# Loading w_hi once for 512 activation columns in a fused attention, mLSTM and SwiGLU layer

## The chip, the cores and the metric

The kernel runs on one core of one Trainium2 chip. The metric is the device time of one execution in microseconds; the profile is of one execution, and its span goes from the first to the last instruction.

## The reference

One layer on 256 tokens of width 1024, all in fp32:

```python
h = rms_norm(x, mix_norm_g)
q_a, k_a, v_a, q_m, k_m, v_m, o_m, i_m, f_m, g_a, g_m = split(h @ w_in)
y_a = causal_attention(q_a, k_a, v_a, slopes)              # 8 heads of 64, one block
q_m, k_m = split(silu(causal_depthwise_conv([q_m, k_m], conv_qk)))   # 4 taps
y_m = head_layer_norm(mlstm(q_m, k_m, v_m, i_m, log_sigmoid(f_m)) * sigmoid(o_m)) * mlstm_norm_g
merged = sigmoid(g_a) * (y_a @ w_out_attn) + sigmoid(g_m) * (y_m @ w_out_mlstm)
x = x + merged @ w_o
h = rms_norm(x, ffn_norm_g)
x = x + (silu(h @ w_ffn_gate) * (h @ w_ffn_up)) @ w_ffn_down         # hidden width 2816
out = rms_norm(x, final_norm_g)
```

## The kernel before

Every large product is made of three matmuls in the type fp32r. An fp32 number is split into a rounded part hi and the remainder lo, and w x is summed as w_hi x_hi + w_hi x_lo + w_lo x_hi. The weights come in chunks of 2048 columns on 128 partitions (1 MB), numbered c in the order in which they are used. Each chunk passes through four engines:

- SyncE issues its load into one of three buffers `w_raw`, after the split of chunk c-3 is done (`lo_ready`).
- ScalarE copies it to `w_hi` (`split_hi`, L404, in the FFN loop L636); it waits for the load and for chunk c-6 to be used, since `w_hi` and `w_lo` are rings of six.
- VectorE subtracts and writes `w_lo` (`split_lo`, L670, in the FFN loop L975).
- TensorE uses it and raises `chunk_used`.

Each engine has its own program, written out by hand, and works through it strictly in order. In the projection ScalarE and VectorE run one loop over c: in iteration c they do what belongs to the middle of the layer at that point, then split chunk c+4, then read the results of a chunk.

The chunks of the projection (L1152 and following), 22 in all:

- 0 to 3: q_m and k_m, feature-major. `tap3` (ScalarE) writes the last convolution tap into `qk_m`, `conv` (VectorE) adds the three others, each of them reading the sum in PSUM. After chunk 1 TensorE does the small product for the eight gate columns (`gates`). In iteration 2, ahead of its split and of `conv(2)`, VectorE works out the gate rows: additions, a wait for ScalarE's exponential and logarithm, two scans (L832 to L852).
- 4 to 7: q_a and k_a, feature-major, copied out by ScalarE (`copy_qk`). After chunk 5 TensorE spreads the gate rows (`gate_columns`); VectorE's iteration 4 begins with a copy that waits for it (L854).
- 8 to 13: v_a, v_m and o_m, token-major, two chunks each. The o block is read by ScalarE with a sigmoid in iteration 15, after the last softmax (`read_block(6, ...)`).
- 14 to 21: the two merge gates, feature-major, read by ScalarE with a sigmoid (`read_gate`).

Between the chunks TensorE does the small matmuls of attention and mLSTM; `scores(3)` stands before chunk 15, `numerators(h)` behind chunks 15 to 18. VectorE's `head_out(h)` follows each of these, and in iteration 19 the normalisation of all heads (L897 to L905), which waits for GpSimd.

A feature-major chunk (`feature_chunk`) holds 8 x 2 weight tiles of 128 x 128. Each tile is the stationary operand, the 256 tokens are the moving one:

```python
for f in range(2):
    o = bank[:, f * S:(f + 1) * S]
    for k in range(KT):
        mm(o, hi[:, w], hT_hi[:, k, :], start=(k == 0), stop=False)
        mm(o, hi[:, w], hT_lo[:, k, :], start=False, stop=False)
        ins = mm(o, lo[:, w], hT_hi[:, k, :], start=False, stop=(k == KT - 1))
```

The chunk's 2 x 256 columns fill one PSUM bank. The projection goes round the four banks of `pp`, so chunk c follows chunk c-4 in its bank: chunk 4 waits for `conv(0)`, chunk 5 for `conv(1)`, and so on (L1173, L1175). The attention works in the four banks of `pa`. A token-major product (`token_product`) has the activations stationary and 512 weight columns moving.

Chunks 22 to 25 are the two out-projections, in the order attention, mLSTM (columns 0 to 511), attention, mLSTM (columns 512 to 1023): the first two go to the four banks of `pa`, the others to `pp`. VectorE multiplies them with the gates and adds (`merge_attention`, `merge_mlstm`), ScalarE and VectorE split the result (`merged_hi`, `merged_lo`). Chunks 26 to 29 are w_o. Then the FFN: a first group of 256 hidden features token-major, then ten groups feature-major (`group`), each with a gate chunk, an up chunk and the down product of the group before. The gate sums alternate between banks 0 and 1 of `pa`, the up sums between 2 and 3. ScalarE takes the silu of the gate, VectorE multiplies by the up sum, and both split the product (`hidden`).

Of the kernel before, what the change touches and what calls it, by code (L numbers as in the profile page):

```python
# [60 lines left out]

def build(nc, x, mix_norm_g, w_in, conv_qk, b_igate, b_fgate, mlstm_norm_g, w_out_attn,
# [11 lines left out]
    with ExitStack() as ctx:  # L74
# [62 lines left out]
        wif = yT_hi[:, :, :].rearrange("p f n -> p (f n)")[:, 0:KT * 100].rearrange("p (k n) -> p k n", k=KT)  # L137
# [9 lines left out]
        sel_r = yT_lo[0:36, 0:2, :].rearrange("p f n -> p (f n)")  # L147
        m_rows = yT_lo[0:36, 2, :]
# [84 lines left out]
        hid_turned = sem("hid_turned")  # L233
        prod_done = sem("prod_done")
# [10 lines left out]
        block = ctx.enter_context(nc.Block())  # L245

# [151 lines left out]
        def _(act):  # L398
# [112 lines left out]
            for c in range(C_OUT):  # L511
# [62 lines left out]
                elif c > 2 * GATES:  # L574
                    read_gate(c - 1)
# [83 lines left out]
        def _(dve):  # L659
# [169 lines left out]
            for c in range(C_OUT):  # L829
# [77 lines left out]
                if c < 4:  # L907
                    conv(c)
# [446 lines left out]
```

## Time and profile before

| what | value |
|---|---|
| median of 3 runs | 401.44 us |
| lowest, highest | 400.5, 401.46 us |
| span of the profiled execution, which is what the profile gives as its own time | 399.2 us |
| TensorE matmuls, share of the span | 387.7 us, 97% |
| TensorE weight loads | 360.9 us, 90% |
| VectorE | 226.0 us, 57% |
| ScalarE | 188.2 us, 47% |
| GpSimd | 36.2 us, 9% |
| mean granted TensorE clock | 0.994 |

Weight loads run beside matmuls. Busy time of a matmul is from its start to its modelled end, and successive matmuls overlap, so their rate is read from their starts. A releaser is what ended an engine's idle time.

### The profile page before, as it was taken

The page shows a single profiled execution, that of the slowest core. Times are in us where ns is not written, and L with a number is a line of the kernel's source. Part 1 is how long each engine was busy: PE and PEld are TensorE (multiplying, and loading weights), DVE is VectorE, ACT ScalarE, POOL GpSimd, SP SyncE. Part 2 cuts the span into 40 slices and gives each one's busy share as a digit, 9 for nine tenths or more (in the row PEclk, how much of TensorE's full clock was granted, in tenths as well). Part 3 has the DMA queues.
Part 4 walks back from the last instruction along what each step waited for, and adds up shares of the span by engine and source line. Part 5 has one row for each costly group of instructions (what it writes and reads, how often), then busy time and mean ns, then how long its engine had stood idle before and what let it go on. Part 6 is the DMA issues. An engine that isn't in the chain of part 4 may idle for free.

```text
span 399.2 us, 6572 instructions
## 1 busy us (share of the span) xinstructions
PE 387.7 (97%) x2749; PEld 360.9 (90%) x2749; DVE 226.0 (57%) x282; ACT 188.2 (47%) x224; POOL 36.2 (9%) x47
## 2 busy tenths in 40 slices
PE   6999999999999999999999999999999999999992
PEld 5799998777999999998899999999999999999982
DVE  1788857648529577587547572552816437263024
ACT  4772996454575445243446353350624416152003
POOL 2897010000000010000100000000000000000002
PEclk9999999999999999999999999999999999999997
DMA  7996276844535489635336665729366292730002
GB/s 266 318 316 211 78 238 223 262 151 120 191 111 181 141 314 318 213 117 196 106 105 225 215 224 182 240 81 313 102 213 205 110 309 65 256 105 0 0 0 105
DMA packets 52620, 71.13 MB, mean 178 GB/s; under 512 B 2260, under 2 KB 41208, under 8 KB 52600
## 3 DMA queue, kind: packets, MB, share of 16 engines
q1 hardware_dynamic: 52456, 70.57, 53.8%
q8 instruction: 16, 0.26, 0.3%
q10 hardware_dynamic: 144, 0.26, 0.2%
q14 instruction: 4, 0.03, 0.0%
HBM read 69.78 MB, written 1.05 MB: 177 GB/s over the span
## 4 chain that ended last, share of the span: by engine, by line
PE 93%; DMA 2%; ACT 1%; SPq 1%; DVE 1%; issue 0%; POOLq 0%; POOL 0%; ACTq 0%
PE pa L1021 10%; PE pa L1020 10%; PE pa L1019 10%; PE pp L1027 9%; PE pp L1028 9%; PE pp L1029 9%; PE pp L1019 7%; PE pp L1020 7%; PE pp L1021 7%; DMA w_raw<-in_w_in 2%; PE pa L1027 2%; PE pa L1029 2%; PE pa L1028 2%; PE pp L1247 1%; PE pp L1246 1%; PE pp L1245 1%
## 5 line engine op out<-in xcount | busy, mean ns | idle before, releaser
L670 DVE TENSOR_TENSOR w_lo<-w_raw,w_hi 128x2048 fp32r<-128x2048 f32 x38 | 86.5, 2289 | 37.3 <-ACT w_hi L404 37.3
L1019 PE MATMUL pa<-hT_hi,w_hi 128*128 128x256 f32 x320 | 90.6, 283 | 0.0
L1021 PE MATMUL pa<-hT_hi,w_lo 128*128 128x256 f32 x320 | 90.6, 283 | 0.0
L1020 PE MATMUL pa<-hT_lo,w_hi 128*128 128x256 f32 x320 | 90.6, 283 | 0.0
L404 ACT ACTIVATE w_hi<-w_raw 128x2048 fp32r<-128x2048 f32 x38 | 72.7, 1915 | 16.8 <-DMA w_raw<-in_w_in 8.3
L1019 PE MATMUL pp<-hT_hi,w_hi 128*128 128x256 f32 x240 | 68.8, 287 | 0.1
L1020 PE MATMUL pp<-hT_lo,w_hi 128*128 128x256 f32 x240 | 67.9, 283 | 0.0
L1021 PE MATMUL pp<-hT_hi,w_lo 128*128 128x256 f32 x240 | 67.9, 283 | 0.0
L1020 PEld LDWEIGHTS pa<-hT_lo,w_hi 128*128 128x128 f32 x320 | 61.4, 192 | 0.4
L1019 PEld LDWEIGHTS pa<-hT_hi,w_hi 128*128 128x128 f32 x320 | 61.4, 192 | 0.3
L1021 PEld LDWEIGHTS pa<-hT_hi,w_lo 128*128 128x128 f32 x320 | 61.4, 192 | 0.0
L975 DVE TENSOR_TENSOR w_lo<-w_raw,w_hi 128x2048 fp32r<-128x2048 f32 x24 | 53.6, 2287 | 8.9 <-ACT w_hi L636 8.9
L636 ACT ACTIVATE w_hi<-w_raw 128x2048 fp32r<-128x2048 f32 x24 | 45.0, 1906 | 3.7 <-PE pp L1029 3.7
L1019 PEld LDWEIGHTS pp<-hT_hi,w_hi 128*128 128x128 f32 x240 | 46.0, 192 | 0.6 <-issue 0.3
L961 DVE TENSOR_TENSOR region_a<-pa,region_a 128x512 f32<-128x512 f32 x10 | 6.9, 692 | 69.3 <-PE pa L1021 69.3
L1020 PEld LDWEIGHTS pp<-hT_lo,w_hi 128*128 128x128 f32 x240 | 46.0, 192 | 0.0
L1021 PEld LDWEIGHTS pp<-hT_hi,w_lo 128*128 128x128 f32 x240 | 46.0, 192 | 0.0
L1027 PE MATMUL pp<-w_hi,yT_hi 128*128 128x512 f32 x88 | 34.4, 390 | 0.0
L1028 PE MATMUL pp<-w_hi,yT_lo 128*128 128x512 f32 x88 | 34.4, 390 | 0.0
L1029 PE MATMUL pp<-w_lo,yT_hi 128*128 128x512 f32 x88 | 34.2, 389 | 0.0
L624 ACT ACTIVATE yT_hi<-region_a 128x512 fp32r<-128x512 f32 x10 | 6.3, 633 | 56.7 <-DVE region_a L961 56.7
L1027 PE MATMUL pp<-w_hi,hT_hi 128*128 128x512 f32 x64 | 25.6, 399 | 0.0
(190 smaller groups left out, 575.7 us busy)
## 6 DMA issues: line engine op xcount, KB each, us to landing
w_raw<-in_w_in SPq DMA_DIRECT2D x21, 1024.0 KB, 5.4
w_raw<-in_w_ffn_gate SPq DMA_DIRECT2D x11, 1024.0 KB, 5.3
w_raw<-in_w_ffn_up SPq DMA_DIRECT2D x11, 1024.0 KB, 6.1
w_raw<-in_w_ffn_down SPq DMA_DIRECT2D x11, 1024.0 KB, 6.6
w_raw<-in_w_o SPq DMA_DIRECT2D x4, 1024.0 KB, 6.0
w_raw<-in_w_out_attn SPq DMA_DIRECT2D x2, 1024.0 KB, 5.0
w_raw<-in_w_out_mlstm SPq DMA_DIRECT2D x2, 1024.0 KB, 5.6
x_sb<-in_x SPq DMA_DIRECT2D x2, 512.0 KB, 3.8
```

What stands on the lines that cost most here:

```text
L404: nc.scalar.activation(w_hi[:, slot_of(c), :], w_raw[:, c % RAW, :], ACT.Copy).then_inc(hi_ready, 1)
L624: nc.scalar.activation(yT_hi[:, 2 * (g % 2):2 * (g % 2) + 2, :], hid[:, g % 2, :].rearrange("p (f n) -> p f n", f=2), ACT.Copy).then_inc(a ...
L636: nc.scalar.activation(w_hi[:, slot_of(c + r), :], w_raw[:, (c + r) % RAW, :], ACT.Copy).then_inc(hi_ready, 1)
L670: nc.vector.tensor_tensor(w_lo[:, slot_of(c), :], w_raw[:, c % RAW, :], w_hi[:, slot_of(c), :].bitcast(F32), ALU.subtract).then_inc(lo_rea ...
L961: nc.vector.tensor_tensor(hid[:, g % 2, :], pa[:, 2 + g % 2, :], hid[:, g % 2, :], ALU.mult).then_inc(prod_done, 1)
L975: nc.vector.tensor_tensor(w_lo[:, slot_of(c + r), :], w_raw[:, (c + r) % RAW, :], w_hi[:, slot_of(c + r), :].bitcast(F32), ALU.subtract).t ...
L1019: mm(o, hi[:, w], hT_hi[:, k, :], start=(k == 0), stop=False)
L1020: mm(o, hi[:, w], hT_lo[:, k, :], start=False, stop=False)
L1021: ins = mm(o, lo[:, w], hT_hi[:, k, :], start=False, stop=(k == KT - 1))
L1027: mm(o, aT_hi[:, k, tok], w_hi[:, s, w], start=start, stop=False)
L1028: mm(o, aT_lo[:, k, tok], w_hi[:, s, w], start=False, stop=False)
L1029: return mm(o, aT_hi[:, k, tok], w_lo[:, s, w], start=False, stop=stop)
```

## The change

`hT` and `yT` now hold hi and lo side by side, so that one matmul with the weights w_hi takes 512 moving columns, x_hi and x_lo, and writes two sums into the two halves of a bank. A second matmul adds w_lo x_hi to the first half. At reading, ScalarE copies the second half out of PSUM and VectorE adds the first half to it. This holds for the feature-major chunks of the projection, for three of the four out-projection chunks and for the ten FFN groups.

A feature-major chunk now fills two banks. The projection has two pairs of banks (`pair_of`), and a chunk waits until the previous use of its pair is read (`proj_free`, `earlier_uses`): chunks 2 to 7 for the sum of chunk c-2, chunk 15 for the reads of the o block, chunks 16 and 17 for the sums of 14 and 15, and so on. `conv`, `sum_qk` and `sum_gate` do the additions on VectorE, behind the split of chunk c+4 in iteration c, those of the gate chunks one iteration later. `tap3` and the convolution taps read the sum from SBUF; `tap3(c)` comes in ScalarE's iteration c+1, ahead of that iteration's split and, in iteration 2, ahead of its exponential. The sigmoid of a gate is a step of its own (`open_gate`).

In the out-projection both attention chunks use `pa` and both mLSTM chunks `pp`. In the FFN the gate always uses banks 0 and 1 of `pa`, the up chunk 2 and 3, so the next gate waits for the addition of the one before (`gate_summed`, `up_summed`). The first FFN group takes gate and up weights in one matmul of 512 columns.

```diff
+def pair_of(c):
+    return c % 2 if c < 2 * FEATURE_MAJOR else (c // 2) % 2 if c < 2 * GATES else (c + 1) % 2
+def earlier_uses(c):
+    first = [n for n in range(c) if n < 2 * FEATURE_MAJOR or n >= 2 * GATES or n % 2 == 0]
+    return sum(pair_of(n) == pair_of(c) for n in first)
...
-        hT_hi = sb("hT_hi", [P, KT, S], F32R)
-        hT_lo = sb("hT_lo", [P, KT, S], F32R)
-        yT_hi = sb("yT_hi", [P, 8, S], F32R)
-        yT_lo = sb("yT_lo", [P, 8, S], F32R)
+        hT = sb("hT", [P, KT, 2, S], F32R)
+        hT_hi, hT_lo = hT[:, :, 0, :], hT[:, :, 1, :]
+        yT = sb("yT", [P, 8, 2, S], F32R)
+        yT_hi, yT_lo = yT[:, :, 0, :], yT[:, :, 1, :]
...
+        def gate_part(c):
+            n = c - 2 * GATES
+            return (region_a, region_b)[n // 4][:, 512 * (n % 4):512 * (n % 4 + 1)]
+        def main_sum(q):
+            return pp[:, 2 * q:2 * q + 2, 0:S]
+        def rest_sum(q):
+            return pp[:, 2 * q:2 * q + 2, S:2 * S]
...
+            def read_rest(c, dst):
+                act.wait_ge(chunk_used, c + 1)
+                nc.scalar.activation(dst, rest_sum(pair_of(c)), ACT.Copy).then_inc(rest_read, 1)
             def tap3(c):
                 b, h = divmod(c, 2)
-                act.wait_ge(chunk_used, c + 1)
+                act.wait_ge(proj_free[pair_of(c)], c // 2 + 1)
                 if c == 0:
                     act.wait_ge(vcol_set, 1)
                 for f in range(2):
                     ft = 4 * b + 2 * h + f
                     col = 4 + 3 * 8 + ft
-                    ins = nc.scalar.activation(qk_m[:, ft, :], pp[:, 2 * (b % 2) + h, f * S:(f + 1) * S],
-                                               ACT.Copy, scale=vcol[:, col:col + 1])
+                    ins = nc.scalar.activation(qk_m[:, ft, :], raw[:, c, f, :], ACT.Copy, scale=vcol[:, col:col + 1])
                 ins.then_inc(tap3_done, 1)
...
+            def read_mix(n):
+                act.wait_ge(chunk_used, C_OUT + n + 1)
+                if n == 2:
+                    act.wait_ge(merged, 1)
+                dst = (mix_sum, ml_sum)[n % 2].rearrange("p (f n) -> p f n", f=4)
+                nc.scalar.activation(dst, (pa, pp)[n % 2][:, :, S:2 * S], ACT.Copy).then_inc(mix_rest, 1)
+            def open_gate(c):
+                act.wait_ge(proj_free[pair_of(c)], earlier_uses(c) + 1)
+                part = gate_part(c)
+                nc.scalar.activation(part, part, ACT.Sigmoid).then_inc(gate_read, 1)
...
+                if c in (1, 2):
+                    tap3(c - 1)
...
+                if c in (3, 4):
+                    tap3(c - 1)
...
-                    tap3(c)
+                    read_rest(c, raw[:, c])
                 elif c < 8:
-                    copy_qk(c)
+                    ft = 4 * (c // 2 - 2) + 2 * (c % 2)
+                    read_rest(c, qk_a[:, ft:ft + 2, :])
                 elif c == 9:
                     read_block(4, lambda t: va[:, t], ACT.Copy)
                 elif c > 2 * GATES:
-                    read_gate(c - 1)
+                    read_rest(c - 1, gate_part(c - 1).rearrange("p (f n) -> p f n", f=2))
+                    if c > 2 * GATES + 1:
+                        open_gate(c - 2)
...
+                nc.scalar.activation(two(hid), pa[:, 0:2, S:2 * S], ACT.Copy).then_inc(gate_rest, 1)
+                act.wait_ge(chunk_used, i * 6 + (C_FFN + 3 * g + 1))
+                nc.scalar.activation(two(up_sum), pa[:, 2:4, S:2 * S], ACT.Copy).then_inc(up_rest, 1)
+                act.wait_ge(gate_summed, i * 2 + g)
+                nc.scalar.activation(hid[:, g % 2, :], hid[:, g % 2, :], ACT.Silu).then_inc(silu_f_done, 1)
...
+                q = pair_of(c)
+                dve.wait_ge(rest_read, c + 1)
+                nc.vector.tensor_tensor(raw[:, c], main_sum(q), raw[:, c], ALU.add).then_inc(proj_free[q], 1)
...
+            def sum_qk(c):
+                q = pair_of(c)
+                ft = 4 * (c // 2 - 2) + 2 * (c % 2)
+                part = qk_a[:, ft:ft + 2, :]
+                dve.wait_ge(rest_read, c + 1)
+                nc.vector.tensor_tensor(part, main_sum(q), part, ALU.add).then_inc(proj_free[q], 1)
...
+            def sum_gate(c):
+                q = pair_of(c)
+                part = gate_part(c).rearrange("p (f n) -> p f n", f=2)
+                dve.wait_ge(rest_read, c - 5)
+                nc.vector.tensor_tensor(part, main_sum(q), part, ALU.add).then_inc(proj_free[q], 1)
...
             def merge_attention(n):
-                if n == 0:
-                    dve.wait_ge(proj_free[0], 10)
-                    dve.wait_ge(proj_free[1], 8)
-                dve.wait_ge(chunk_used, C_OUT + 2 * n + 1)
+                dve.wait_ge(gate_read, 2 * n + 2)
+                dve.wait_ge(mix_rest, 2 * n + 1)
+                total = mix_sum.rearrange("p (f n) -> p f n", f=4)
+                nc.vector.tensor_tensor(total, pa[:, :, 0:S], total, ALU.add).then_inc(mix_summed, 1)
+                dve.wait_ge(mix_summed, n + 1)
                 part = region_a[:, 1024 * n:1024 * (n + 1)]
-                nc.vector.tensor_tensor(part, (pa, pp)[n][:, 0:2, :].rearrange("p b n -> p (b n)"), part, ALU.mult)
+                nc.vector.tensor_tensor(part, mix_sum, part, ALU.mult)
             def merge_mlstm(n):
+                dve.wait_ge(gate_read, 2 * n + 6)
                 dve.wait_ge(chunk_used, C_OUT + 2 * n + 2)
                 for b in range(2):
                     part = slice(512 * (2 * n + b), 512 * (2 * n + b + 1))
-                    link(nc.vector.tensor_tensor(region_b[:, part], (pa, pp)[n][:, 2 + b, :], region_b[:, part],
-                                                 ALU.mult))
+                    total = main_sum(b)
+                    gate = region_b[:, part].rearrange("p (f n) -> p f n", f=2)
+                    if n == 0:
+                        dve.wait_ge(mix_rest, 2)
+                        summed = ml_sum[:, 512 * b:512 * (b + 1)].rearrange("p (f n) -> p f n", f=2)
+                        link(nc.vector.tensor_tensor(summed, total, summed, ALU.add))
+                        total = summed
+                    link(nc.vector.tensor_tensor(gate, total, gate, ALU.mult))
...
+                elif c < 8:
+                    sum_qk(c)
+                elif c > 2 * GATES:
+                    sum_gate(c - 1)
...
+                dve.wait_ge(gate_rest, i * 2 + g)
+                nc.vector.tensor_tensor(two(hid), pa[:, 0:2, 0:S], two(hid), ALU.add).then_inc(gate_summed, 1)
+                dve.wait_ge(up_rest, i * 2 + g)
+                nc.vector.tensor_tensor(two(up_sum), pa[:, 2:4, 0:S], two(up_sum), ALU.add).then_inc(up_summed, 1)
                 dve.wait_ge(silu_f_done, i * 2 + g + 1)
-                dve.wait_ge(chunk_used, i * 6 + (C_FFN + 3 * g + 1))
-                nc.vector.tensor_tensor(hid[:, g % 2, :], pa[:, 2 + g % 2, :], hid[:, g % 2, :], ALU.mult
+                dve.wait_ge(up_summed, i * 2 + g)
+                nc.vector.tensor_tensor(hid[:, g % 2, :], up_sum[:, g % 2, :], hid[:, g % 2, :], ALU.mult
...
+            def split_product(bank, hi, lo, xT, k, start, stop):
+                mm(bank, hi, xT[:, k], start=start, stop=False)
+                return mm(bank[:, 0:S], lo, xT[:, k, 0, :], start=False, stop=stop)
+            def feature_chunk(c, banks):
                 s = slot_of(c)
                 hi, lo = w_hi[:, s, :], w_lo[:, s, :]
                 for f in range(2):
-                    o = bank[:, f * S:(f + 1) * S]
                     for k in range(KT):
                         w = slice(k * 256 + f * P, k * 256 + (f + 1) * P)
-                        mm(o, hi[:, w], hT_hi[:, k, :], start=(k == 0), stop=False)
-                        mm(o, hi[:, w], hT_lo[:, k, :], start=False, stop=False)
-                        ins = mm(o, lo[:, w], hT_hi[:, k, :], start=False, stop=(k == KT - 1))
+                        ins = split_product(banks[f], hi[:, w], lo[:, w], hT, k, k == 0, k == KT - 1)
                 return ins
...
                 elif b < FEATURE_MAJOR or b >= GATES:
-                    if b >= GATES:
-                        pe.wait_ge(proj_free[b % 2], 2 * (b // 2 - 1) - 1 + h)
-                    elif b >= 2:
-                        pe.wait_ge(conv_step, 6 * (c - 3))
-                    if c == 1:
-                        pe.wait_ge(vcol_set, 1)
-                    feature_chunk(c, pp[:, 2 * (b % 2) + h, :]).then_inc(chunk_used, 1)
+                    q = pair_of(c)
+                    if c > 1:
+                        pe.wait_ge(proj_free[q], earlier_uses(c))
+                    feature_chunk(c, (pp[:, 2 * q, :], pp[:, 2 * q + 1, :])).then_inc(chunk_used, 1)
...
-                banks = (pa, pp)[n]
                 for m in range(2):
+                    banks = (pa, pp)[m]
                     if n == 0 and m == 0:
                         pe.wait_ge(ya_lo_set, 4)
                         pe.wait_ge(num_read, H_M)
+                        pe.wait_ge(ym_lo_set, 2)
                     elif n == 0:
-                        pe.wait_ge(ym_lo_set, 2)
-                    elif m == 0:
                         pe.wait_ge(proj_free[0], 10)
+                        pe.wait_ge(proj_free[1], 9)
                     else:
-                        pe.wait_ge(proj_free[1], 8)
+                        pe.wait_ge((mix_summed, merged)[m], 1 + m)
                     c = C_OUT + 2 * n + m
                     s = slot_of(c)
                     pe.wait_ge(lo_ready, c + 1)
...
                         pe.wait_ge(m_lo_set, 2 * h + 2)
+                        pe.wait_ge(mix_summed, 2)
...
+                    w = (slice(None), slice(s, s + 2), slice(256 * k, 256 * (k + 1)))
+                    o = pa[:, 2 + t, :]
+                    mm(o, hT_hi[:, k, tok], w_hi[w], start=(k == 0), stop=False)
+                    mm(o, hT_lo[:, k, tok], w_hi[w], start=False, stop=False)
+                    ins = mm(o, hT_hi[:, k, tok], w_lo[w], start=False, stop=(k == KT - 1))
+                    if t == 0 and k == 4:
+                        turn(rb_t[:, 1], (pp[:, 0, :], pp[:, 1, :]), 6)
...
-                        pe.wait_ge((silu_f_done, prod_done)[r], i * 2 + (g - 1))
-                    feature_chunk(c + r, pa[:, 2 * r + g % 2, :]).then_inc(chunk_used, 1)
+                        pe.wait_ge((gate_summed, up_summed)[r], i * 2 + (g - 1))
+                    elif r == 1:
+                        pe.wait_ge(prod_done, 1)
+                    feature_chunk(c + r, (pa[:, 2 * r, :], pa[:, 2 * r + 1, :])).then_inc(chunk_used, 1)
```

## Rows read from the trace of the kernel before

**Rows 1.** The page, first part: busy time, share of the span and instructions
```profile
PE 387.7 (97%) x2749; PEld 360.9 (90%) x2749; DVE 226.0 (57%) x282; ACT 188.2 (47%) x224; POOL 36.2 (9%) x47
```

**Rows 2.** The table of waits for TensorE: total, times, longest
```profile
PE pa L1038 <- DVE region_b L800: 2.0, 1, 2.0
```

**Rows 3.** Timeline of TensorE, 299 to 304 us: start, duration, line, shapes
```profile
299.79 0.39 PE L1028 MATMUL pp<-w_hi,yT_lo 128*128 128x512 f32 x1
...
301.60 0.28 PE L1019 MATMUL pa<-hT_hi,w_hi 128*128 128x256 f32 x1
...
303.99 0.28 PE L1021 MATMUL pa<-hT_hi,w_lo 128*128 128x256 f32 x1
```

**Rows 4.** Costliest groups by line and shape: count, busy, mean ns, idle before
```profile
L1019 PE MATMUL pa<-hT_hi,w_hi 128*128 128x256 f32 x320 | 90.6, 283 | 0.0
...
L1019 PE MATMUL pp<-hT_hi,w_hi 128*128 128x256 f32 x240 | 68.8, 287 | 0.1
...
L620 ACT ACTIVATE region_a<-pa 128x512 f32<-128x512 f32 x10 | 6.0, 597 | 39.0 <-PE pa L1021 39.0
...
L777 DVE TENSOR_TENSOR region_b<-pp,region_b 128x512 f32<-128x512 f32 x2 | 1.4, 688 | 0.6 <-PE pp L1247 0.6
...
L770 DVE TENSOR_TENSOR region_a<-pa,region_a 128x1024 f32<-128x1024 f32 x1 | 1.2, 1224 | 1.1 <-PE pa L1247 1.1
```

**Rows 5.** Timeline of VectorE, 26 to 46 us
```profile
26.37 2.36 DVE L670 TENSOR_TENSOR w_lo<-w_raw,w_hi 128x2048 fp32r<-128x2048 f32 x1 [1.28 <-ACT w_hi L404]
28.65 2.42 DVE L691 SCALAR_TENSOR_TENSOR region_a<-pp,vcol,region_a 128x255 f32<-128x255 f32 x6
...
35.53 0.46 DVE L834 TENSOR_SCALAR o_sb<-pa,b_if 4x256 f32<-4x256 f32 x1
...
40.30 0.41 DVE L843 SCALAR_TENSOR_TENSOR o_sb<-o_sb 4x256 f32<-4x256 f32 x1 [2.21 <-ACT o_sb L522]
...
43.96 2.29 DVE L670 TENSOR_TENSOR w_lo<-w_raw,w_hi 128x2048 fp32r<-128x2048 f32 x1
```

**Rows 6.** Timeline of ScalarE, 26 to 30 us
```profile
26.24 0.82 ACT L431 ACTIVATE region_a<-pp,vcol 128x256 f32<-128x256 f32 x2
...
27.77 1.91 ACT L404 ACTIVATE w_hi<-w_raw 128x2048 fp32r<-128x2048 f32 x1
```

**Rows 7.** Timeline of TensorE: what stands at the places the prediction speaks of
```profile
8.95 1.32 PE L1038 MATMUL pa<-ident,region_b 128*128 128x128 f32 x8 [2.03 <-DVE region_b L800]
...
26.81 0.28 PE L1019 MATMUL pp<-hT_hi,w_hi 128*128 128x256 f32 x1
...
49.94 0.73 PE L1065 MATMUL pa<-yT_lo 36*128 36x256 f32 x4
...
50.94 0.38 PE L1019 MATMUL pp<-hT_hi,w_hi 128*128 128x256 f32 x1
...
110.82 0.38 PE L1019 MATMUL pp<-hT_hi,w_hi 128*128 128x256 f32 x1
...
139.78 0.36 PE L1019 MATMUL pp<-hT_hi,w_hi 128*128 128x256 f32 x1
...
391.71 0.39 PE L1029 MATMUL pp<-w_lo,yT_hi 128*128 128x512 f32 x1
```

**Rows 8.** Timeline of ScalarE, 115 to 117 us: the reads of the o block
```profile
115.67 1.09 ACT L463 ACTIVATE o_sb<-pp 128x512 f32<-128x512 f32 x2
```

**Rows 9.** Timeline of VectorE, 140 to 147 us
```profile
140.06 0.16 DVE L743 SCALAR_TENSOR_TENSOR den<-pa,rcol 128x2 f32<-128x2 f32 x1 [2.23 <-PE pa L1139]
...
144.20 2.14 DVE L903 TENSOR_SCALAR o_sb<-o_sb,mv,lnr 128x128 f32<-128x128 f32 x8 [2.13 <-POOL lnr L392]
```

**Rows 10.** Windows: busy time of the five engines, granted clock, DMA share, GB/s
```profile
8.00:12.00 4.00, 2.87 (x17) 1.81 (x17) 3.63 (x6) 2.36 (x4) 0.73 (x1) 1.00 1.10 361
...
393.00:394.00 1.00, 0.00 (x0) 0.00 (x0) 1.00 (x2) 0.59 (x2) 0.26 (x1) 1.00 0.27 102
394.00:395.00 1.00, 0.00 (x0) 0.00 (x0) 0.27 (x2) 0.00 (x0) 0.84 (x2) 0.52 0.43 160
```

More of the change, by code:

```diff
@@ L615, in hidden, with two @@
             def hidden(i, g):
+                def two(ap):
+                    return ap[:, g % 2, :].rearrange("p (f n) -> p f n", f=2)
                 act.wait_ge(chunk_used, i * 6 + (C_FFN + 3 * g))
@@ L919, in _ @@
             split_lo(C_WO)
+            sum_gate(C_OUT - 1)
             split_lo(C_WO + 1)
@@ L1156, in _ @@
                 if c == 0:
-                    hh, hl, lh = (w_hi, hT_hi), (w_hi, hT_lo), (w_lo, hT_hi)
-                    order = ((hh, 0), (hl, 0), (hh, 1), (hl, 1), (lh, 1), (lh, 0))
                     for f in range(2):
-                        for n, ((w_part, x_part), half) in enumerate(order):
-                            pe.wait_ge(((first_half_hi, hi_ready) if w_part is w_hi else
-                                        (first_half_lo, lo_ready))[half], 1)
-                            pe.wait_ge(hT_hi_set if x_part is hT_hi else hT_lo_set, 3 + half)
+                        w = [slice(k * 256 + f * P, k * 256 + (f + 1) * P) for k in range(KT)]
@@ L1166, in _ @@
+                        for half in range(2):
+                            pe.wait_ge((first_half_hi, hi_ready)[half], 1)
+                            pe.wait_ge(hT_lo_set, 3 + half)
                             for k in range(4 * half, 4 * half + 4):
-                                ins = mm(pp[:, 0, f * S:(f + 1) * S],
-                                         w_part[:, 0, k * 256 + f * P:k * 256 + (f + 1) * P], x_part[:, k, :],
-                                         start=(n == 0 and k == 0), stop=(n == 5 and k == 3))
+                                mm(pp[:, f, :], w_hi[:, 0, w[k]], hT[:, k], start=(k == 0), stop=False)
@@ L1170, in _ @@
+                        for half in (1, 0):
+                            pe.wait_ge((first_half_lo, lo_ready)[half], 1)
+                            for k in range(4 * half, 4 * half + 4):
+                                ins = mm(pp[:, f, 0:S], w_lo[:, 0, w[k]], hT_hi[:, k, :], start=False,
+                                         stop=(half == 0 and k == 3))
                     ins.then_inc(chunk_used, 1)
                 elif b < FEATURE_MAJOR or b >= GATES:
-                    if b >= GATES:
-                        pe.wait_ge(proj_free[b % 2], 2 * (b // 2 - 1) - 1 + h)
-                    elif b >= 2:
-                        pe.wait_ge(conv_step, 6 * (c - 3))
```

115 lines of the change are left out of this document (61 added, 54 removed).

## The prediction

> **What bounds the kernel now.** I began with the busy shares. TensorE has work for 387.7 of 399.2 us, VectorE and ScalarE for about half of it [rows 1]; the table of waits gives TensorE's matmuls one wait of 2.0 us in the norm at the start and nothing that matters later [rows 2]. So the kernel is as long as its matmuls, and a gain has to come out of their spacing. The timeline of TensorE gives that spacing, start to start: the eight 512-column matmuls from 299.79 to 301.60 take 0.226 us each, the twenty 256-column ones from 301.60 to 303.99 take 0.1195 us each [rows 3]. Doubling the columns adds 0.107 us, so each matmul carries about 12.7 ns that do not depend on its columns (2 x 0.1195 - 0.2263).
>
> Then I read VectorE's and ScalarE's timelines, because the change makes TensorE wait for them [rows 5 to 9]. Both run a fixed program in order, and in the first 55 us and around the last gate chunks VectorE is far behind TensorE. Nobody sees it today: with four banks in turn, chunk 4 waits only for the convolution of chunk 0, and chunk 6 for that of chunk 2.
>
> **What is saved.** A triple of 256-column matmuls becomes one of 512 columns and one of 256: 0.346 instead of 0.359 us, 12.7 ns less. Of such triples there are 256 in the 16 feature chunks of the projection (240 in the rows and the 16 of chunk 0, which has a line of its own), 320 in the FFN loop [rows 4] and 48 in three of the four out-projection chunks (4 x 4 weight tiles each, by the code). That is 624 x 12.7 ns = 7.9 us. The first FFN group turns 96 matmuls of 256 columns into 48 of 512: 0.6 us. Together 8.5 us, 0.2 us for each chunk, if a mixed sequence keeps both spacings. The Trainium skill (TensorE: Matmul & The Clock Gate, Back-to-back issue gap) states N/2.4 + 2.5 ns for a warm isolated matmul; by that the 672 matmuls saved would be worth an estimated 1.7 us. The rows show 12.7 ns, and the sum goes by them.
>
> **What is added.** Each bank pair needs a ScalarE copy (0.6 us, as other 512-column copies here) and a VectorE add (0.69 us, as the 512-element operations of L777 [rows 4]). Neither engine is short of time in the sum. What counts is when a pair is free. A chunk now takes two banks, two pairs go round, and chunk c waits for the sum of chunk c-2, which stands in VectorE's program behind the split of chunk c+2. I follow that program with the durations of before.
>
> *Chunk 2.* The gate matmuls now end near 26.6 (26.81 less 0.2 [rows 7]). The sum of chunk 0 can start only after the split that runs to 28.65 [rows 5], so it ends at 29.35. Stall 2.8 us.
>
> *Chunk 3.* tap3 now reads the sum, so it starts at 29.4 and takes 0.8 (ScalarE's 0.82 pair); the split of chunk 5 on ScalarE moves behind it, to 32.0 [rows 6]. VectorE: taps 30.25 to 32.65, split 34.9, sum of chunk 1 at 35.6. TensorE ends chunk 2 at 34.95. Stall 0.65 us. Chunk 3 ends at 41.15.
>
> *Chunk 4.* It needs the sum of chunk 2. Ahead of that on VectorE stand tap3(1) by ScalarE (to 36.4), taps (to 38.85), then the whole gate-row block, from 35.53 to 40.30 and on to 43.96 in the rows [rows 5], 8.4 us with ScalarE's exponential, table load and logarithm inside it: to 47.25. Then the split of chunk 6, 2.3: 49.55. Then the sum: 50.25. Stall 9.1 us. Even without any delay upstream the sum could not be there before 46.95 (the split that starts at 43.96 ends at 46.25), so this wait doesn't hang on small errors.
>
> *Chunk 5.* tap3(2) waits for that sum, then the split on ScalarE (to 52.85), VectorE's taps and split (55.75) and the sum: 56.45, TensorE is there at 55.8. Stall 0.65.
>
> *Chunk 6.* VectorE's next instruction is the copy of the gate columns (0.17 us), which waits for TensorE's small matmuls behind chunk 5 (1.0 us, 49.94 to 50.94 [rows 7]), then split 8 and the sum of chunk 4: 0.17 + 2.29 + 0.69. Stall 3.2 us. Chunks 7 to 14: sums in time by 1 us or more, no stall; there the shift is 14 to 15 us.
>
> *Chunk 15.* It shares its pair with the o block. Today it goes to another bank and starts at 110.82 [rows 7], as the scores of the last head pair end. Now it waits for both sigmoid reads of the o block, which ScalarE does after the last softmax and a table load, until 116.76 (115.67 + 1.09) [rows 8]. Stall 5.9 us.
>
> *Chunks 16 to 19.* Head output, split and sum take 5.0 us after the numerators, a chunk 5.55: no stall. *Chunk 20* needs the sum of chunk 18. In the rows VectorE has head output from 140.06, a wait for GpSimd, and the normalisation to 146.3; then split 2.2 and sum 0.7: 149.2 [rows 9]. TensorE would be there at 139.78 + 5.76 = 145.55 [rows 7]. Stall 3.7 us.
>
> *Out-projection.* The fourth chunk waits for the merge of the second: copy 1.1, twice 0.69 x 3, in all 5.3, against the third chunk of 5.55: just hidden. But the merge runs on into the w_o product: from the end of the second chunk VectorE and ScalarE need 1.1 + 4.2 + 1.4 (low halves) + 2.25 (split) + 1.2 + 1.2 (sum, product of 1024 [rows 4]) + 2.25 + 2.8 + 1.4 = 17.85 us, TensorE 5.55 + 5.76 + 5.45 = 16.75. Stall about 1.2 with semaphores. Its cover before was about 1.1 us.
>
> *FFN.* Here I charge nothing. ScalarE already waits 3.9 us for each gate chunk (39.0 in all [rows 4]), so it and VectorE arrive in time. The gate's sum is ready 1.4 us after its chunk and needed 11 us after; the up chunk's sum too. The hidden values come 1.4 us later than now and have two chunks and more as cover; the last group has one down product of 5.4 us over a chain of 3.5. The reads before chunk 0 shift too: 512-column matmuls need both halves of h, 0.7 us later, but chunk 1 starts with its own split at 19.07 as now.
>
> Stalls: 2.8 + 0.65 + 9.1 + 0.65 + 3.2 + 5.9 + 3.7 + 1.2 = 27.2 us. Less 8.5: +18.7 us.
>
> **The clock.** TensorE's last matmul ends near 392.1 and the granted clock, 1.00 (2.4 GHz) until 394, is 0.52 in the microsecond after it, which is the lower level, 1.2 GHz; the pause of 2.0 us before 8.95 left it at 1.00 [rows 2, 7, 10]. So stalls above about 2 us can put it at half, above all the four of 3.2, 9.1, 5.9 and 3.7 us. How long it stays there once matmuls run again no row shows. Bounds: nothing, and a whole chunk at half speed, 5.5 us more, after each of the four: 22 us. I take the return to be about as slow as the fall, 2 to 3 us of work at half speed, which loses 1.5 us per stall: 6.0, less 0.65 that falls into the wait of chunk 5: 5.3 us. The Trainium skill (TensorE: Matmul & The Clock Gate, The HAM clock gate) says the same in kind: idle halves the clock and sustained work gives it back; the fall in rows 10 agrees.
>
> **Sum.** 18.7 + 5.3 = +24.0 us. The durations are of an execution with span 399.2; the median of the runs is 401.44, 2.2 above, which I take as unchanged: 401.4 + 24.0 = 425.4, say 425.
>
> **The rivals.**
> 1. *Forecast:* VectorE's late sums hold TensorE, mainly at chunks 4, 15, 6 and 20, and the clock falls in most of these. 425, own range 421 to 430. Chance 0.66.
> 2. *Same waits, clock stays up or returns at once.* For it: the 2 us pause did nothing. Against it: 9.1 us is four times as long. 401.4 + 18.7 = 420. Chance 0.14.
> 3. *Same waits, clock slow for whole chunks.* 401.4 + 18.7 + 22 = 442. Chance 0.07.
> 4. *The saving is not there.* The mixed sequence could space as before, because a matmul's fixed part moves to the following one. 401.4 + 27.2 + 5.3 = 434; with 1.7 us saved 432. Against it: both spacings show the same fixed part. Chance 0.06.
> 5. *Fewer waits:* one of the chains is shorter than I read, most likely that of chunk 15 or of chunk 20 (5.9 and 3.7, with their clock cost 3): 412 to 413. Chance 0.04.
> 6. *The other side, faster.* TensorE stays fed, as in the FFN it will, and all 8.5 us count: 393. It would need the sum of chunk 2 to be ready when chunk 3 ends. The kernel is faster only if all stalls stay under 8.5 us; as chunk 4 alone cannot start before 46.95 where TensorE could be there at 37.7, the first 50 us would already have used it up. Chance 0.03, for an error in reading the order.
>
> Under 0.3% (1.2 us) nothing can be told from no change. Faster 0.03, within it 0.01, slower 0.96. The range takes rivals 1 and 2 with most of 4: 416 to 433.
>
> **What the profile after would show.** The table of waits should have TensorE rows released by VectorE additions: about 9 us before chunk 4, then 3 each at chunks 2 and 6, 4 at chunk 20, 1 in the w_o product, and 6 us released by the ScalarE sigmoid read. Chunks without a wait should take 5.55 us (0.226 + 0.120 per weight tile), an FFN group 0.4 us less than its 96 x 0.1195 + 24 x 0.2263 = 16.9. The FFN loop should have no TensorE wait; one there would be worth ten times its size and is the quickest way to make this too low. The windows after each long stall should show a clock under 1.00 for 2 to 3 us. It is too high if VectorE's first 50 us run faster than now, or if the clock never falls.

## The result, and the profile after

The changed kernel takes 433.4 us (433.28 to 434.76, 4 runs) where the kernel before takes 401.4 (400.5 to 401.46, 4 runs): a ratio of 1.0815 [1.0795, 1.0835]. It is 32.0 us slower. I had forecast 24 us slower, 425, with a range of 416 to 433, so it lies just outside.

The page of the changed kernel, its span, busy shares and granted clock, answers to [rows 1]:

```profile
span 431.2 us, 5314 instructions
PE 395.8 (92%) x2077; PEld 334.7 (78%) x2077; DVE 254.8 (59%) x322; ACT 208.1 (48%) x259; POOL 36.6 (8%) x47
PEclk9988798999997999699999999999999999999998
PE 78%; DVE 10%; ACT 4%; DMA 4%; issue 2%; SPq 1%; POOL 1%; POOLq 0%; DVEq 0%; ACTq 0%
```

TensorE is now busy for 92% of the span, not 97, and VectorE holds 10% of the chain that ended last. The row PEclk has a dip in the slices behind each long wait. Next is the table of waits of TensorE's matmuls, which answers to [rows 2] (columns: us in total, times, longest):

```profile
PE pp L1109 <- DVE region_b L741: 10.9, 2, 7.5
PE pp L1109 <- ACT o_sb L498: 6.0, 1, 6.0
PE pp L1109 <- DVE region_b L768: 3.6, 1, 3.6
PE pp L1109 <- DVE region_b L761: 3.2, 1, 3.2
...
PE pa L1125 <- DVE hT L866: 0.7, 1, 0.7
```

L1109 is the wide matmul of a feature chunk. L741 is the sum of a convolution chunk (it releases chunks 2 and 4), L498 the sigmoid read of the o block (chunk 15), L768 the sum of chunk 18 (chunk 20), L761 the sum of chunk 4 (chunk 6). These are the five chunks named before the run, with the releasers named. VectorE's timeline shows why the largest comes (start, duration, idle before and its releaser); it answers to [rows 5]:

```profile
26.38 2.29 DVE L726 TENSOR_TENSOR w_lo<-w_raw,w_hi 128x2048 fp32r<-128x2048 f32 x1 [2.09 <-ACT w_hi L437]
28.59 0.68 DVE L741 TENSOR_TENSOR region_b<-pp,region_b 128x512 f32<-128x512 f32 x1
...
39.57 0.47 DVE L916 TENSOR_SCALAR o_sb<-pa,b_if 4x256 f32<-4x256 f32 x1
...
44.08 0.41 DVE L925 SCALAR_TENSOR_TENSOR o_sb<-o_sb 4x256 f32<-4x256 f32 x1 [2.21 <-ACT o_sb L560]
...
47.74 2.29 DVE L726 TENSOR_TENSOR w_lo<-w_raw,w_hi 128x2048 fp32r<-128x2048 f32 x1
50.06 0.69 DVE L741 TENSOR_TENSOR region_b<-pp,region_b 128x512 f32<-128x512 f32 x1
```

The gate rows begin at 39.57 and end at 47.7, then comes the split of chunk 6, and only then the sum of chunk 2, which ends at 50.75. The prediction had 50.25. TensorE's timeline shows what the wait does to the matmuls behind it:

```profile
50.90 0.76 PE L1109 MATMUL pp<-hT,w_hi 128*128 128x512 f32 x1 [7.46 <-DVE region_b L741]
51.46 0.41 PE L1110 MATMUL pp<-hT,w_lo 128*128 128x256 f32 x1
...
54.88 0.63 PE L1109 MATMUL pp<-hT,w_hi 128*128 128x512 f32 x1
55.30 0.32 PE L1110 MATMUL pp<-hT,w_lo 128*128 128x256 f32 x1
55.47 0.40 PE L1109 MATMUL pp<-hT,w_hi 128*128 128x512 f32 x1
55.70 0.28 PE L1110 MATMUL pp<-hT,w_lo 128*128 128x256 f32 x1
55.82 0.39 PE L1109 MATMUL pp<-hT,w_hi 128*128 128x512 f32 x1
```

A wide matmul is charged 0.63 us and a pair takes 0.64 (start to start) until 55.4, then 0.40 and 0.35. The windows of 5 us after the waits give the granted clock in the column behind POOL. In four of them it is 0.50 or 0.51, the lower level, 1.2 GHz, as in [rows 10]; in 70:75 it is 0.75, as the clock comes back in the middle of that window:

```profile
30.00:35.00 5.00, 5.00 (x17) 4.31 (x16) 4.75 (x7) 2.50 (x3) 4.73 (x4) 0.51 0.60 204
50.00:55.00 5.00, 4.10 (x13) 3.55 (x14) 4.00 (x9) 3.19 (x4) 0.00 (x0) 0.50 0.64 213
70.00:75.00 5.00, 5.00 (x25) 4.30 (x24) 2.89 (x2) 3.58 (x3) 0.78 (x2) 0.75 0.50 176
135.00:140.00 5.00, 4.55 (x14) 3.90 (x15) 2.86 (x3) 2.59 (x3) 0.00 (x0) 0.50 0.02 3
175.00:180.00 5.00, 4.36 (x13) 3.76 (x14) 5.00 (x4) 2.43 (x2) 0.00 (x0) 0.50 0.79 248
```

By the timeline the slow stretches last 5.3, 4.5, 3.6, 5.2 and 5.9 us: 24.5 us in which work is done at 0.35/0.64 of the speed, so about 11 us lost. The 2.4 of them behind chunk 2 only shorten the waits of chunks 3 and 4, which VectorE sets, and 0.6 behind chunk 4 takes the place of a wait of chunk 5: some 8 net.

The FFN loop has no TensorE wait. Its pairs, at 2.4 GHz, answer to [rows 3]:

```profile
300.04 0.39 PE L1109 MATMUL pa<-hT,w_hi 128*128 128x512 f32 x1
300.27 0.28 PE L1110 MATMUL pa<-hT,w_lo 128*128 128x256 f32 x1
300.38 0.40 PE L1109 MATMUL pa<-hT,w_hi 128*128 128x512 f32 x1
...
301.09 0.40 PE L1109 MATMUL pa<-hT,w_hi 128*128 128x512 f32 x1
```

From 300.38 to 301.09 two pairs take 0.71 us. The period of a group, from one first gate matmul to the next, is 16.79 us (300.04 to 316.83), where before it was 16.98 (301.60 to 318.58). I had expected 0.4 less; it is 0.19, so 0.19/32 = 5.9 ns for each of a group's 32 pairs, not 12.7.

In the projection the same sequence has two paces. These are two pairs of chunk 14, 0.69 us, which is the 0.346 a pair of the forecast:

```profile
123.80 0.39 PE L1109 MATMUL pp<-hT,w_hi 128*128 128x512 f32 x1
...
124.49 0.39 PE L1109 MATMUL pp<-hT,w_hi 128*128 128x512 f32 x1
```

Chunks 16 and 18 keep that pace too, while chunks 17, 19 and 21, with the same code, take 0.353 or 0.354.

One more difference stands behind TensorE's last matmul. The last output transfer, which ScalarE issues, takes 0.9 us longer. This is its row in the table of transfers, before and after; the last number is the time from issue to landing:

```profile
out_x<-region_b ACTq DMA_DIRECT2D x1, 256.0 KB, 2.7
```

```profile
out_x<-region_b ACTq DMA_DIRECT2D x1, 256.0 KB, 3.6
```

The edit doesn't touch this transfer, and no run shows why it is slower. It takes 3.6 us in `warm`, `early`, `front_only` and `gates_only` as well and 2.7 in the four other experiments.

### The profile page after: what moved, and what is told of

The parts are those of the page before. It is cut to its first block, busy times and chain, and to the rows that moved or that the text cites. A ratio compares the mean times of both kernels' runs of the same rounds, so it can differ in the third digit from the quotient of the medians.

```text
span 431.2 us, 5314 instructions
## 1 busy us (share of the span) xinstructions
PE 395.8 (92%) x2077; PEld 334.7 (78%) x2077; DVE 254.8 (59%) x322; ACT 208.1 (48%) x259; POOL 36.6 (8%) x47
## 4 chain that ended last, share of the span: by engine, by line
PE 78%; DVE 10%; ACT 4%; DMA 4%; issue 2%; SPq 1%; POOL 1%; POOLq 0%; DVEq 0%; ACTq 0%
PE pa L1109 18%; PE pp L1109 12%; PE pa L1110 9%; PE pp L1125 8%; PE pp L1127 8%; PE pp L1126 8%; PE pp L1110 6%; DMA w_raw<-in_w_in 4%; DVE w_lo L726 3%; DVE region_a L750 1%; ACT w_hi L437 1%; PE pa L1379 1%; PE pa L1381 1%; PE pa L1380 1%; DVE region_a L861 1%
## 5 line engine op out<-in xcount | busy, mean ns | idle before, releaser
L1109 PE MATMUL pp<-hT,w_hi 128*128 128x512 f32 x240 | 96.5, 438 | 23.7 <-DVE region_b L741 10.9
L1109 PE MATMUL pa<-hT,w_hi 128*128 128x512 f32 x320 | 113.5, 399 | 0.0
L1110 PE MATMUL pa<-hT,w_lo 128*128 128x256 f32 x320 | 89.8, 281 | 0.0
L1109 PEld LDWEIGHTS pp<-hT,w_hi 128*128 128x128 f32 x240 | 50.6, 211 | 37.2 <-DVE w_lo L726 18.7
L1110 PE MATMUL pp<-hT,w_lo 128*128 128x256 f32 x240 | 72.1, 300 | 0.0
L1109 PEld LDWEIGHTS pa<-hT,w_hi 128*128 128x128 f32 x320 | 60.1, 188 | 14.8
L1110 PEld LDWEIGHTS pa<-hT,w_lo 128*128 128x128 f32 x320 | 60.4, 189 | 0.4
L1110 PEld LDWEIGHTS pp<-hT,w_lo 128*128 128x128 f32 x240 | 50.7, 211 | 0.0
L1125 PE MATMUL pp<-w_hi,yT 128*128 128x512 f32 x88 | 34.6, 393 | 0.0
L1126 PE MATMUL pp<-w_hi,yT 128*128 128x512 f32 x88 | 34.3, 390 | 0.0
L1125 PE MATMUL pp<-w_hi,hT 128*128 128x512 f32 x64 | 25.6, 399 | 0.0
L1126 PE MATMUL pp<-w_hi,hT 128*128 128x512 f32 x64 | 24.9, 389 | 0.0
```

Source lines behind the costliest of these rows:

```text
L1109: mm(bank, hi, xT[:, k], start=start, stop=False)
L1110: return mm(bank[:, 0:S], lo, xT[:, k, 0, :], start=False, stop=stop)
L1125: mm(o, aT_hi[:, k, tok], w_hi[:, s, w], start=start, stop=False)
L1126: mm(o, aT_lo[:, k, tok], w_hi[:, s, w], start=False, stop=False)
```

## The experiments

Each ratio is to the kernel before on the same chip.

### The clock by itself

`warm` is the changed kernel with extra matmuls, whose results nobody reads, in front of the five waits, so that TensorE stays at work while VectorE and ScalarE are late.

```diff
+filler = {2: (3, 14), 4: (3, 38), 6: (0, 13), 15: (1, 25), 20: (2, 15)}
 for c in range(C_OUT):
...
+    for _ in range(filler[c][1]):
+        mm(pa[:, filler[c][0], :], hT_hi[:, 0, 0:P], hT[:, 0], start=True, stop=True)
```

> The changed kernel with filler matmuls on TensorE ahead of the waits of chunks 2, 4, 6, 15 and 20 (14, 38, 13, 25 and 15 of 512 columns into banks that nothing reads), so that it is busy while it would wait; the sums come no earlier. Theory: the late sums are one cost and the clock's fall in the waits another, of about 11 us (what the chunks behind the five long waits took over their usual length in the trace of the changed kernel, against the 5.3 us of the prediction). Then the granted clock stays at 1.00, the chunks behind the waits take 5.65 us, and the time falls from 433.4 to 421 to 424 us. Rival: the chunks behind the waits were slow for another reason, and the half clock beside them costs nothing by itself because VectorE sets the pace there; then it stays at 431 to 434 us, with the waits longer by what the chunks are shorter.

Measured: 425.7 us (425.49 to 427.42), 1.0621 [1.0595, 1.0648], granted clock 0.996. The return from half speed costs 433.4 - 425.7 = 7.7 us. That is less than the 11 I had expected to get back, because part of the slow stretches had only filled waits, and so the time lies above the 421 to 424 expected. From the start of chunk 1 to that of chunk 21 the two traces differ by 8.1 us (166.7 and 158.6). TensorE's timeline of `warm` around chunk 4:

```profile
42.25 8.80 PE L1257 MATMUL pa<-hT 128*128 128x512 f32 x38
51.39 0.47 PE L1109 MATMUL pp<-hT,w_hi 128*128 128x512 f32 x1 [0.34 <-DVE region_b L741]
51.69 0.28 PE L1110 MATMUL pp<-hT,w_lo 128*128 128x256 f32 x1
51.81 0.40 PE L1109 MATMUL pp<-hT,w_hi 128*128 128x512 f32 x1
```

Filler and wait end 9.14 us after 42.25, when the chunk could have started; the forecast was 9.1. With the clock up, this kernel shows the waits that the sum was about. From the starts of the chunks, forecast in brackets: chunk 2 3.3 (2.8), chunk 3 1.1 (0.65), chunk 4 9.1 (9.1), chunk 5 0.6 (0.65), chunk 6 3.2 (3.2), chunk 15 6.1 (5.9), chunk 20 3.8 (3.7), w_o 0.9 (1.2). Together 28.1 against 27.2. So the waits were right, and the rival with whole chunks at half speed, 22 us, is out.

### The waits, moved away one group at a time

`early` puts the sums, and ScalarE's copies that go before them, where their data are ready: those of chunks 2 to 6 ahead of the gate rows, the taps or the split, the sum of chunk 18 ahead of the normalisation, the read of the o block ahead of the last softmax. `front_only` and `gates_only` have one half of this each.

```diff
 if c == 2:
+    sum_raw(2)
     dve.wait_ge(gates_done, 1)
...
+    sum_raw(3)
...
+if c in (3, 4, 5):
+    sum_qk(c + 1)
...
+read_block(6, lambda t: o_t[:, t], ACT.Sigmoid)
 ya_hi(1)
 softmax_exp(3)
-read_block(6, lambda t: o_t[:, t], ACT.Sigmoid)
...
 head_out(3)
+sum_gate(18)
 dve.wait_ge(lnr_set, 1)
```

> The changed kernel with the same work in another order: ScalarE's copies and VectorE's sums of chunks 2 to 6 stand ahead of the splits and of the gate rows instead of behind them, the sum of chunk 18 ahead of the normalisation of the heads, and the reads of the o block ahead of the last softmax. Theory: only the place of the sums in the queues makes TensorE wait. The wait of 7.5 us before chunk 4, of 6.0 before 15, of 3.6 before 20 and of 3.2 before 6 should be gone or under 1 us each, that before chunk 2 (3.4 us) stays and may cost 2 to 3 us of half clock behind it. Gain left from the wider matmuls: 672 x 6 to 7 ns, about 4.4 us. Sum: 401.4 - 4.4 + 3.4 + 2.5 + about 1.5 of small waits = 404, range 400 to 409. Rival: two bank pairs are too few wherever the sums stand, because the two copies per chunk load VectorE and ScalarE and other waits take their place; then 415 us or more.

Measured: 406.2 us (405.1 to 407.48), 1.0133 [1.0103, 1.0162], clock 0.993. The order alone takes 27.2 of the 32 us away. What is left in its table of waits:

```profile
PE pp L1123 <- DVE region_b L745: 4.7, 3, 3.0
...
PE pp L1123 <- DVE region_a L778: 1.2, 1, 1.2
PE pa L1139 <- DVE hT L876: 0.8, 1, 0.8
```

That is chunk 2 with 3.0 us, two of 0.8, one of 1.2 for the sum of a gate chunk and 0.8 in w_o, 6.7 us in all (7.4 from the starts), which is more than the 4.7 that the wide matmuls save. In this order, too, two pairs of banks don't feed TensorE.

> The changed kernel with the early sums of chunks 2 to 6 alone; chunks 15 and 20 wait as in the changed kernel. Theory: each wait costs its length and its own stretch of half clock and they add up. Gone: 7.5 (chunk 4) + 3.2 (chunk 6) of wait and 2.0 + 1.6 of slow matmuls behind them, 14.3 us; new small waits of about 2 us, as in the kernel with all sums early. 433.4 - 14.3 + 2 = 421 us, range 419 to 423. Rival: what is freed in front is given back at chunk 15 or 20 by queues that now have less time; then 424 us or more, with the waits there longer than 6.0 and 3.6.

Measured: 418.7 us (417.75 to 419.89), 1.0452 [1.0432, 1.0472]: 14.7 less than the changed kernel, and 0.3 under the range, since the 2 us of new small waits didn't come: chunk 5 waits 0.25 us. In the table of waits chunk 15 and chunk 20 keep theirs to the tenth:

```profile
PE pp L1123 <- ACT o_sb L498: 6.0, 1, 6.0
PE pp L1123 <- DVE region_b L779: 3.6, 1, 3.6
PE pp L1123 <- DVE region_b L746: 3.2, 2, 3.0
```

> The changed kernel with the other half alone: o block read ahead of the last softmax, sum of chunk 18 ahead of the normalisation. Gone: 6.0 + 3.6 of wait and 2.4 + 2.8 of slow matmuls behind them, 14.8 us: 418.6 us, range 417 to 421. Together with the run before the two gains should make up the 27.3 us of the kernel with all sums early. Rival: the two extra loads of ScalarE's function table and the sum in front of the normalisation move other waits; then less than 12 us are gained.

Measured: 422.0 us (421.35 to 422.66), 1.0531 [1.0514, 1.0549]: 11.4 less, and so above the range of 417 to 421; it is also under the 12 us that the rival named. The waits of chunks 15 and 20 are gone, but new ones stand in the table, and that of the convolution sums grew:

```profile
PE pp L1109 <- DVE region_b L740: 12.8, 2, 8.6
PE pp L1109 <- DVE region_b L760: 3.2, 1, 3.2
...
PE pp L1109 <- DVE region_a L767: 1.2, 1, 1.2
```

The 1.2 us is chunk 16, whose sum is the next to be late once chunk 15 is on time. The edit touches nothing before chunk 15, yet the waits there grew. VectorE's timeline of this profiled execution has two slow entries there:

```profile
30.99 3.54 DVE L749 SCALAR_TENSOR_TENSOR region_a<-region_b,vcol,region_a 128x255 f32<-128x255 f32 x6 [0.98 <-ACT region_a L469]
34.46 3.17 DVE L725 TENSOR_TENSOR w_lo<-w_raw,w_hi 128x2048 fp32r<-128x2048 f32 x1
```

In the changed kernel the same taps took 2.94 and the same split 2.28 us. With a weight load that came 0.7 us later this puts the chain to chunk 4 back by 2.0 us (52.90 instead of 50.90). What VectorE lost, GpSimd gained: its two instructions of L412, which run beside the split, took 2.44 us here and 3.67 in the traces of the changed kernel, `warm`, `early` and `front_only`, where the split took 2.28. That the two slow each other is my reading, and no run tests it. These 2.0 us and chunk 16's wait, 1.4 from its start, are the 3.4 that are missing from the 14.8 expected. Only one of the four executions has a trace; it was the fastest of them. Why the engines ran so here stays open. The two parts together gained 26.1, `early` 27.2: they add up within about a microsecond.

### The saving by itself

`ffn_only` is the kernel before with the change in the FFN loop and its first group alone; chunks 0 to 29 stay as they were.

```diff
-feature_chunk(c + r, pa[:, 2 * r + g % 2, :]).then_inc(chunk_used, 1)
+paired_chunk(c + r, (pa[:, 2 * r, :], pa[:, 2 * r + 1, :])).then_inc(chunk_used, 1)
```

> The kernel before with the FFN part of the change alone (512 columns in the ten groups and in the first one; projection and out-projection as before). Theory: no wait is added here and a pair of matmuls takes 0.353 us where the three took 0.360, so 320 x 6.5 ns + 48 x 13 ns = 2.7 us less: 398.7 us, ratio 0.993. Rival, the prediction's own term: 12.7 ns each, 4.7 us less: 396.7 us. Second rival: the groups gain nothing, since what a group saves is lost where TensorE waits for the next additions: 401.4 us.

Measured: 398.9 us (398.63 to 398.95), 0.994 [0.9924, 0.9957], period of a group 16.79 us, as in the changed kernel. As expected, this part alone is a gain, of 2.4 us. By the forecast's spacing it would have been 320 x 12.7 ns and 0.6, 4.7 us.

`ffn_grouped` runs the eight wide matmuls of a half chunk and then its eight narrow ones:

```diff
     for k in range(KT):
         w = slice(k * 256 + f * P, k * 256 + (f + 1) * P)
         mm(banks[f], hi[:, w], hT[:, k], start=(k == 0), stop=False)
+    for k in range(KT):
+        w = slice(k * 256 + f * P, k * 256 + (f + 1) * P)
         ins = mm(banks[f][:, 0:S], lo[:, w], hT_hi[:, k, :], start=False, stop=(k == KT - 1))
```

> As ffn_only, but in each half of a feature-major chunk the eight 512-column matmuls come first and then the eight of 256 columns, instead of in turn. If the alternation of the two widths is what makes a pair 0.353 us instead of 0.226 + 0.120 = 0.346, the groups lose another 32 x 6.5 ns = 0.2 us each and the time is 2.1 us under ffn_only, 396.6 us. Rival: the extra 6 to 7 ns belong to the 512-column matmul with activations of this layout (or to its weight load) wherever it stands; then the time is that of ffn_only within 0.3 us and the 512-column matmuls in a row are spaced by more than 0.226 us.

Measured: 397.0 us (396.69 to 397.07), 0.9894 [0.9877, 0.991], period 16.61. TensorE's timeline (successive matmuls of one kind are one entry):

```profile
299.64 1.07 PE L1053 MATMUL pa<-hT,w_hi 128*128 128x512 f32 x4
300.55 1.11 PE L1056 MATMUL pa<-hT,w_lo 128*128 128x256 f32 x8
301.50 2.00 PE L1053 MATMUL pa<-hT,w_hi 128*128 128x512 f32 x8
303.34 0.40 PE L1056 MATMUL pa<-hT,w_lo 128*128 128x256 f32 x2
```

Eight narrow ones take 0.95 us (300.55 to 301.50), eight wide ones 1.84: 0.349 a pair. So in the FFN the order has a price: strictly in turn a pair costs some 4 to 6 ns more.

`ffn_twos` asks what it hangs on, the number of changes between the forms or the lone narrow matmul between two wide ones: two wide, two narrow, in turn.

```diff
+for j in range(0, KT, 2):
+    for k in (j, j + 1):
...
+        mm(banks[f], hi[:, w], hT[:, k], start=(k == 0), stop=False)
+    for k in (j, j + 1):
...
+        ins = mm(banks[f][:, 0:S], lo[:, w], hT_hi[:, k, :], start=False, stop=(k == KT - 1))
```

> As ffn_only, with two 512-column matmuls, then two of 256 columns, in turn: half as many changes of width as in ffn_only. If a change of width costs a fixed time, half of the 1.85 us between ffn_only (398.85) and ffn_grouped (397.0) is won: 397.9 us, and a group of four matmuls takes 0.699 us. Rival: only the return to a wide matmul right behind one narrow one costs, and two narrow ones in a row hide it; then 397.0 us and 0.692 us.

Measured: 396.6 us (396.11 to 397.03), 0.9888 [0.9871, 0.9904], period 16.59. It has four times the changes of form of `ffn_grouped` and is as fast:

```profile
300.44 0.62 PE L1054 MATMUL pa<-hT,w_hi 128*128 128x512 f32 x2
300.90 0.40 PE L1057 MATMUL pa<-hT,w_lo 128*128 128x256 f32 x2
301.14 0.63 PE L1054 MATMUL pa<-hT,w_hi 128*128 128x512 f32 x2
```

Two pairs take 0.70 us and not 0.71. My own theory, a price for each change, falls, as four times the changes cost nothing more. The rival fits the time (it said 397.0) but not the spacing: four matmuls take 0.697 us, as in groups of eight, and not its 0.692. Nor can the lone narrow matmul be the whole cause, since chunks 14, 16 and 18 of the changed kernel have it and take 0.346 a pair. Chunk 3, with the same code in each, takes 0.353 in the changed kernel and 0.347 in `warm` and `early`. What decides between the two paces no run here shows; in every run with the pairs in turn the FFN had the slower one.

### All parts that should pay

`late_grouped` has chunks 0 to 7 as before, and from chunk 14 on everything of the change, grouped, with the o block read and sum 18 early.

```diff
+narrow_chunk(c, pp[:, 2 * (b % 2) + h, :]).then_inc(chunk_used, 1)
 elif b >= GATES:
+    pe.wait_ge(proj_free[q], earlier_uses(c))
+    feature_chunk(c, (pp[:, 2 * q, :], pp[:, 2 * q + 1, :])).then_inc(chunk_used, 1)
```

> A version that may beat both: chunks 0 to 7 as in the kernel before (four banks in turn, three matmuls of 256 columns), chunks 14 to 21, three out-projection chunks and the FFN with 512 columns, wide matmuls first and narrow ones after, and the reads of the o block and the sum of chunk 18 early as in gates_only. Theory: no wait in front, under 1.5 us of waits behind, gain 12.7 ns for 128 + 48 + 320 + 48 matmuls = 6.9 us, less about 1 us of waits at the w_o product: 401.3 - 6.9 + 1 = 395.4 us. Rival: the gate chunks and the out-projection bring new waits that eat their 2.2 us; then it is at the 397.0 us of ffn_grouped or above.

Measured: 398.4 us (397.83 to 398.58), 0.9938 [0.9922, 0.9955]: no better than the FFN part alone, 3 us above the forecast and 1.4 above `ffn_grouped`, as the rival had it. Its timeline shows what eats the saving of the gate chunks and the out-projection:

```profile
118.29 0.93 PE L1123 MATMUL pp<-hT,w_hi 128*128 128x512 f32 x3 [1.23 <-DVE region_a L760]
```

Chunk 16 waits 1.2 us for the sum of chunk 14 (1.5 from its start); w_o waits 0.7 (0.9). Against `ffn_grouped` these parts save 1.7 us of matmul time, so the two waits take back more. The best kernels of the study are `ffn_twos` and `ffn_grouped`, 4.6 and 4.3 us below the one before; between the two there is no difference clear of their scatter.

## Why the prediction was right in kind and missed in size

**The mechanism held.** It was the first rival: VectorE's late sums at chunks 2, 4, 6 and 20 and ScalarE's late read at chunk 15, with a fallen clock behind them. By `warm` the waits sum to 28.1 us against 27.2. Chunks 3 and 5 showed no wait in the changed kernel, as their predecessors ran at half speed and took that time; they do in `warm`. Moving the sums and the read gave 27.2 us back, the clock's share among them, so the order of VectorE's and ScalarE's programs is the cause of most of the loss.

**The saving was mis-sized.** "Together 8.5 us, 0.2 us for each chunk, if a mixed sequence keeps both spacings": the FFN's doesn't keep them, and of the projection's chunks only about half do. A group of the FFN saves 5.9 ns a pair. In `warm` the 14 chunks 1 to 7 and 14 to 20 save 1.8 us together (133.1 us from chunk 1 to chunk 21 before, 158.6 with 27.2 of waits in `warm`), 8 ns a pair. All stretches of the trace together save 4.7 us, 3.8 less than forecast. The steps for the FFN waits were right: none. The rival that had no saving at all names the time, 432 to 434, but by luck: more than half of the saving was there, and what makes up for it is clock, waits and the output transfer. The Trainium skill (TensorE: Matmul & The Clock Gate, Back-to-back issue gap) gives N/2.4 + 2.5 ns for a warm isolated matmul; by that a pair would take an estimated 0.325 us. The trace has 0.353 or 0.346 in turn and 0.349 in groups, and the measurement decides.

**The clock was mis-sized.** "I take the return to be about as slow as the fall, 2 to 3 us of work at half speed": the five returns took 3.6 to 5.9 us, and all five waits, that of chunk 2 too, brought one. Measured net 7.7 us against 5.3, so 2.4 more. The third rival had 22 and the second nothing; the truth lay between, nearer the forecast. The Trainium skill (TensorE: Matmul & The Clock Gate, HAM oscillation) describes a kernel in which the wait for a load before each tile lets the clock fall, so that the tile runs slow; here the same is seen behind five waits, though these are for another engine's reads (granted clock 0.50 and 0.51).

**Left out.** The output transfer at the end, 0.9 us longer, stands in no sum of the prediction. Two slips of the working change nothing: the terms of the w_o chain add up to 17.8, not 17.85, and the table of waits has a second early wait of TensorE, 1.6 us for GpSimd's `ident`, in both kernels.

**The account.** 401.3 + 28.1 (waits) - 4.7 (saving) + 0.9 (transfer) = 425.6 with the clock up, `warm` has 425.7. The changed kernel's 7.7 above that are the clock's, by that comparison alone. Against the forecast: 3.8 (saving), 2.4 (clock), 0.9 (waits) and 0.9 (transfer) are the 8 us. The range reached 433 for the missing saving by itself, with 2 us less for the clock than there were; it did not take both terms off together.

**Open.** What sets the pace of a mixed sequence, 0.346 or 0.353 us a pair; why the last transfer is slower; why two of the four executions of `early` took 407.1 and 407.5 us. The other two took 405.1 and 405.3, which 401.3 + 7.4 - 4.7 + 0.9 = 404.9 explains. The granted clock was 0.987 and 0.990 in the slower two, 0.993 and 0.992 in the faster two, which would fit a clock that fell behind a wait there; only a faster one has a trace.

## What to carry to other kernels

A matmul that takes twice the columns takes twice the banks, so count what the halved ring of banks now waits for: not how busy the reading engine is, but where the read stands in its program. Price a wait at TensorE like those here (3.2 to 7.5 us) at its length plus what the lower clock loses behind it: five cost 7.7 us net, 11 before overlaps. Before counting a saving per instruction, measure the mixed sequence as it will run; and a change that pays in one loop (here the FFN, 2.4 us, or 4.6 in twos) is tried there alone first.

## What the runs showed of the hardware

- Matmuls of 512 and 256 columns in turn, each with its own weight load, take 0.353 us a pair in every FFN group measured, and 0.346 or 0.353 in chunks of the projection. In the FFN, in groups of eight the two forms take 0.119 and 0.230 us, 0.349 together; two and two in turn 0.35. In groups of eight the wide ones are 4 ns slower than the 0.226 of [rows 3].
- The clock after a wait near 3 us goes either way. In `early` chunk 2 starts after 3.02 us at full speed, in `front_only` the same chunk after 2.96 us at half, by the first matmul of each timeline:

```profile
29.68 0.47 PE L1123 MATMUL pp<-hT,w_hi 128*128 128x512 f32 x1 [3.02 <-DVE region_b L745]
```

```profile
29.72 0.76 PE L1123 MATMUL pp<-hT,w_hi 128*128 128x512 f32 x1 [2.96 <-DVE region_b L746]
```

- It can also fall after the matmuls have begun again: chunk 6 starts with 0.47 us, and from 68.9 on its wide matmuls take 0.63, until 72.5.
- How long the return takes does not follow the wait: 4.5 us behind the wait of 7.5, 5.9 behind that of 3.6.
